# Hybrid sparse and dilated attention layer: QK-norm one item later in the projection, attention tiles from last to first

## The reference, cut to what matters

```
xn = rms_norm(x, norm_gain)
proj = xn @ w_in                       # 1024 -> 4420 columns
qa, ka, va, za, qi, ki, wi, qb, kb, vb, zb = split(proj)
qa, ka, qb, kb = per-head rms_norm (64 columns a head) times a gain
# A: indexer scores every causal key, keeps the 256 best of each query
score = sum_h relu(qi_h . ki) * wi_h ;  keep = top_k(score, 256)
a_out = softmax(qa . ka / 8 + bias, over keep) @ va
# B: dilated windows (128,1), (512,4), (2048,16), merged by their denominators
b_out = dilated_attention(qb, kb, vb)
out = x + concat(a_out * silu(za), b_out * silu(zb)) @ w_out
```

## Time and profile before

| | |
|---|---|
| median of 7 runs | 8387.62 us (8355.07 to 8503.0) |
| the profiled execution | 8384.74 us, its slowest core's span 8383.2 us |
| spans of the 8 cores | 8317.9 to 8383.2 us, granted clock 0.683 to 0.692 |
| busy in the span | TensorE 58%, VectorE 59%, ScalarE 67%, POOL 7% |
| projection | to about 1838 us |
| attention A of the first batch | 1846 to 4497 us, of the second 5104 to 7767 us |
| attention B and output projection | 4501 to 5098 us, and from 7770 us to the end |

### The profile page before, as it was taken

The page is one execution under the profiler, slowest core; times in us unless marked ns, Lnnn a source line. Parts: engine busy times, 40 slices in busy tenths (PEclk is TensorE's granted clock), DMA queues, the critical chain, the costliest instruction groups (busy, mean ns, idle before and its releaser), DMA issues. The chain is left out here.

```text
span 8383.2 us, 132302 instructions; the slowest of 8 cores (8317.9 to 8383.2 us)
## 1 busy us (share of the span) xinstructions
PE 4861.0 (58%) x40338; PEld 3177.5 (38%) x40338; DVE 4987.0 (59%) x9513; ACT 5648.6 (67%) x8477; POOL 598.8 (7%) x974
## 2 busy tenths in 40 slices
PE   3777667762455555555555962345555555556586
PEld 1332223321333444444444721233444444446452
DVE  2221222217777778777882655777877787775445
ACT  3655556755777788887885812677887888789551
POOL 2111111210000000000001100000000000000210
PEclk9877889985555556666667776555555566667769
DMA  5111212220000000000002474000000000000448
GB/s 159 68 64 61 68 62 75 74 92 24 23 16 28 18 21 20 21 23 22 25 2 74 143 247 147 26 15 26 19 20 33 21 12 14 24 23 3 129 141 281
DMA packets 249943, 494.53 MB, mean 59 GB/s; under 512 B 82016, under 2 KB 145408, under 8 KB 241568
## 3 DMA queue, kind: packets, MB, share of 16 engines
q1 hardware_dynamic: 192928, 314.06, 12.7%
q0 software_dynamic: 56320, 172.01, 5.5%
HBM read 313.99 MB, written 171.95 MB: 58 GB/s over the span
## 5 line engine op out<-in xcount | busy, mean ns | idle before, releaser
L194 DVE TENSOR_SCALAR_CACHE_REDUCE nm_u<-sc_u,cand_u 128x128 bf16<-128x128 f32 (+15 forms) x960 | 2245.2, 2339 | 1.7 <-issue 1.7
L185 ACT ACTIVATE nm_u<-sc_u,cand_u 128x256 bf16<-128x256 f32 (+15 forms) x960 | 2029.1, 2114 | 200.1 <-DVE cand_u L202 179.6
L176 PE MATMUL pb<-VA_s_u,pbuf_u 128*128 128x65 bf16 x8448 | 799.3, 227 | 2183.7 <-ACT pbuf_u L185 2179.9
L176 PEld LDWEIGHTS pb<-VA_s_u,pbuf_u 128*128 128x128 bf16 x8448 | 560.9, 117 | 2476.3 <-issue 2472.0
L176 PE MATMUL pb<-ident_u,nm_u 128*128 128x128 bf16 x6528 | 1389.9, 286 | 10.4 <-DVE nm_u L194 10.4
L176 PE MATMUL pb<-Qi_u,KaT_s_u 128*128 128x128 bf16 x6528 | 1376.5, 284 | 0.6 <-issue 0.2
L202 DVE SCALAR_TENSOR_TENSOR sc_u<-rbuf_u,wi_all_u,sc_u 128x512 f32<-128x512 f32 (+3 forms) x1152 | 813.7, 706 | 726.2 <-ACT rbuf_u L185 509.9
L185 ACT ACTIVATE pbuf_u<-pb,b_u 128x512 bf16<-128x512 f32 (+2 forms) x1728 | 1085.3, 664 | 4.7 <-PE pb L176 4.4
L185 ACT ACTIVATE rbuf_u<-pb 128x512 f32<-128x512 f32 (+3 forms) x1152 | 591.6, 560 | 560.9 <-PE pb L176 310.2
L176 PEld LDWEIGHTS pb<-ident_u,nm_u 128*128 128x128 bf16 x6528 | 862.8, 132 | 49.2 <-issue 37.2
L176 PEld LDWEIGHTS pb<-Qi_u,KaT_s_u 128*128 128x128 bf16 x6528 | 853.1, 131 | 7.9 <-issue 1.6
(11 more groups left out here) (100 smaller groups left out, 6672.3 us busy)
## 6 DMA issues: line engine op xcount, KB each, us to landing
Bres<-res_u POOLq DMA_DIRECT2D x192, 260.0 KB, 2.4
rr_u<-Bres SPq DMA_DIRECT2D x192, 260.0 KB, 7.4
xs_u<-x SPq DMA_DIRECT2D x64, 512.0 KB, 4.0
xf_u<-x SPq DMA_DIRECT2D x64, 512.0 KB, 5.3
out<-ot_u POOLq DMA_DIRECT2D x64, 512.0 KB, 7.1
vt_u<-Vb SPq DMA_DIRECT2D x192, 130.0 KB, 2.3
wst_u<-w_in SPq DMA_DIRECT2D x8, 2048.0 KB, 10.8
Va<-vst_u POOLq DMA_DIRECT2D x64, 130.0 KB, 2.6
```

The lines of the kernel that those rows point to most:

```text
L176: return lambda e: e.matmul(o, lhsT=l, rhs=r, start=start, stop=stop)
L185: return lambda e: e.activation(out=o, in_=i, func=func, scale=scale, **kw)
L194: return lambda e: e.tensor_scalar(out=o, in0=i, scalar1=s1, scalar2=s2, op0=op0, **kw)
```

## The change

Three things. In the projection the norm of an f item is split: its matmuls and the Square stay, and the rest (the `bones` matmul, Ln, Exp, multiply, store, or the copy of the other f items) is emitted behind the matmuls and the Square of the next f item. For that pf rotates over three PSUM tiles (pb0, pb1, pb3) and pS is pb2 alone. The items of a group are put in another order: the 8 VA and VB items stand between the first f items, then the other 11 f items in a row, then the 8 ZA and ZB items in a row; what is pending is emitted behind each ZA or ZB item. And the pairs of attention A go from m = 15 down to 0: A(15) alone, then A(m-1) with B(m), then B(0) alone.

```
@@ -430,7 +430,7 @@
-                pf = pb[kf % 2]
+                pf = (pb[0], pb[1], pb[3])[kf % 3]
...
@@ -438,8 +438,10 @@
                 if gc is not None:
-                    sq_, sd2, rs2, pS = sqb[kf % 2], sdb[kf % 2], rsb[kf % 2], pb[2 + kf % 2]
+                    sq_, sd2, rs2, pS = sqb[kf % 2], sdb[kf % 2], rsb[kf % 2], pb[2]
                     P.op("act", _act(sq_[:], pf[:], ACTF.Square), reads=[pf], writes=[sq_])
+                yield
+                if gc is not None:
                     P.op("pe", _mm(pS[:], bones[:], sq_[:], True, True), reads=[bones, sq_], writes=[pS])
...
@@ -486,16 +488,16 @@
+            pend = [None]
             for q in range(len(groups)):
+                vit = [("t", tt * 4 + j) for tt in range(4) for j in (0, 2)]
+                git = [("t", tt * 4 + j) for tt in range(4) for j in (1, 3)]
                 items = []
-                fi, ti = 0, 0
-                while fi < len(FM) or ti < 16:
-                    if fi < len(FM):
-                        items.append(("f", fi))
-                        fi += 1
-                    if ti < 16:
-                        items.append(("t", ti))
-                        ti += 1
+                for fi in range(len(FM)):
+                    items.append(("f", fi))
+                    if fi < len(vit):
+                        items.append(vit[fi])
+                items += git
...
                     if kind == "f":
-                        fm_item(q, v)
+                        gnew = fm_item(q, v)
+                        next(gnew)
+                        if pend[0] is not None:
+                            for _ in pend[0]:
+                                pass
+                        pend[0] = gnew
                     else:
                         tm_item(q, v // 4, v % 4)
+                    if (n_ == len(items) - 1 or (kind == "t" and v % 2 == 1)) and pend[0] is not None:
+                        for _ in pend[0]:
+                            pass
+                        pend[0] = None
...
@@ -712,12 +723,14 @@
-                for _ in stageA(0):
+                order = list(range(NP_ - 1, -1, -1))
+                for _ in stageA(order[0]):
                     pass
-                for m in range(NP_):
-                    ga = stageA(m + 1) if m + 1 < NP_ else iter(())
+                for oi, m in enumerate(order):
+                    mn = order[oi + 1] if oi + 1 < NP_ else None
+                    ga = stageA(mn) if mn is not None else iter(())
                     gbb = stageB(m)
-                    ua = unitsA(m + 1) if m + 1 < NP_ else 0
+                    ua = unitsA(mn) if mn is not None else 0
```

## The result

| | before | after |
|---|---|---|
| median of the runs compared | 8392.1 us (31 runs) | 8174.93 us (12 runs, 8112.75 to 8225.47) |
| ratio, 95% interval | | 0.9738, 0.9711 to 0.9765 |
| span of the profiled execution | 8383.2 us | 8145.4 us |
| table loads | 259 | 84 |
| core 6: first `kiT_u` load (projection done) | 1808.9 us | 1591.9 us |

A forecast was written before the change was run, and what follows sets the result against it. No engine was full: TensorE and ScalarE waited for each other in the projection, ScalarE and VectorE were nearly level in attention A. 8384.7 - 248 (projection) + 34 (attention) = 8171, forecast 8175 us, 8-in-10 range 8040 to 8320.

The forecast's parts named there:

- Table loads, 83: Projection, ScalarE: grouping the Silu leaves 83 table loads for 259, 226 us less ScalarE work.
- A late group, 74.5 us: Projection group without bias tables: 66.5 us of TensorE work plus waits, 74.5 for 88.1 us, 218 us in all.
- f items without a t item: Late group's last eight f items: TensorE waits for the norm chain to free pf, 3.3 us a group.
- among the Silu: Late group's Silu stretch: ScalarE's loads, Silu, Ln and Exp hold the fourth item's PSUM tile, 2.9 us of TensorE wait.
- Bias tables, 30 us: Projection's early groups: more TensorE items beside the first table's Exp hide its DMA trip, 30 us gained in all.
- Projection together, -248 us: Whole projection: 218 us from the groups and 30 from the bias tables, with bounds of 170 and 290 us.
- The three rotating tiles, the shared pS and the extra lists cost nothing more.: Projection: the new PSUM tile use and item lists add no cost, 0 us, unless ScalarE falls behind.
- The ends of attention, +107 a batch: Attention A's unpaired stages: A(15) 230 and B(0) 20 us replace A(0) 55 and B(15) 88, +107 us a batch.
- The middle, -90 a batch: Attention A's fifteen pairs: shorter by 90 us a batch, between ScalarE's -57 and VectorE's -169.
- 4 to 8 us shorter: Sign in attention A: each pair 4 to 8 us shorter than the pair of the same two numbers before.
- The lower clock at 0.81: Rival, projection: denser matmuls lower the mean clock to 0.81, late groups gain 2 us, total 8360 us; chance 0.09.
- fall to 0.70: Rival, projection: waits bring the mean clock to 0.70, projection +75 us, total 8494 us; chance 0.05.

The follow-up runs named there:

- The late Exp: The kernel after, with the Exp that ends a bias table issued at least 8 items behind the rest of its table: 8066.69 us, ratio 0.9624.
- the flush ahead of the Silu: The kernel after, with the last pending norm finished ahead of a group's first Silu item instead of behind it: 8147.36 us, ratio 0.9722.
- the late Exp and old items: The kernel before plus split norm, three tiles and bias Exp 8 items late; attention A up and down 8044.72 us, ascending 8098.95 us.

## Why the prediction came out

8175 us was forecast and 8174.93 measured. That the two agree so closely is luck: single runs of after lie between 8113 and 8225 us, and two terms were off and made up for each other.

- **Table loads, 83.** There are 84. That they were worth little, since TensorE binds, was said and is now shown from both sides: 207 fewer gave no gain that can be measured, 245 left standing took none of it away. What was wrong is the reading of the earlier trace rows, where I had the Square standing behind a load as the reason for the wait. The Square alone takes nearly that long.
- **A late group, 74.5 us.** 74.9 on core 6, term by term from the waits in four groups: f items without a t item 3.0 us (forecast 3.3), among the Silu 2.75 (2.9), for `sdb` 0.8 where 1.8 were allowed for other work of ScalarE. Against that TensorE's work is 68.4 us for 66.5: the matmuls that take 3.49 us for 1.89 are most of it, a term that the sum did not have. Two items of that chain take 5.07 us (5.03), from the start of the first of these rows to that of the last, in the timeline of after, core 6:

```profile
1480.87 1.89 PE L176 MATMUL pb<-xnT_u,W_u 128*128 128x512 bf16 x8
...
1484.00 1.89 PE L176 MATMUL pb<-xnT_u,W_u 128*128 128x512 bf16 x8 [1.03 <-DVE fst_u L202]
...
1485.94 1.89 PE L176 MATMUL pb<-xnT_u,W_u 128*128 128x512 bf16 x8
```

  The 0.25 + 0.52 us that the prediction calls the Square in this chain are not its time: the earlier trace rows have 0.60 for the Square, and 0.47 from the start of `bones` to that of the Ln. Against core 6's own late groups it is 12.9 us each, 206 in all for my 218.
- **Bias tables, 30 us.** This is the term that failed. Three tables cost 116.4 - 87.7 = 28.7 us a group before and 102.5 - 74.9 = 27.6 after: some 10 us in all. I had argued that four items of TensorE's work beside the Exp hide more of it than two. For two of the tables they do: in the early group shown above, ScalarE stands 8.9 and 10.5 us at their Exp, and TensorE waits at most 1.3 us at a time for `sdb` or `fst`. But the third Exp falls among the Silu, which I had seen and not priced high enough. The timeline of that group, after, core 6:

```profile
902.94 1.28 ACT L185 ACT_TABLE_LOAD   x1 [7.22 <-DMA NBf_u<-Rscr]
904.23 0.42 ACT L185 ACTIVATE EB_u<-NBf_u 128x256 bf16<-128x256 f32 x1
...
906.70 4.85 PE L176 MATMUL pb<-W_u,xnT_u 128*128 128x512 bf16 x11 [6.79 <-ACT gst_u L185]
```

  TensorE stands for 6.8 us behind it, and its waits for `gst` are 9.6 us in this group for 2.75 in a late one. That takes back what the two others give. The late Exp shows that this wait was the price.
- **Projection together, -248 us.** -217 on core 6, whose clock was not held (last section), -197 on core 3, which the forecast was made for.
- **"The three rotating tiles, the shared pS and the extra lists cost nothing more."** True and not enough. I had given the tiles no price for their absence; the third decides between -2.7% and +3.3%.
- **The ends of attention, +107 a batch.** +104 (226.3 and 20.9 for 230 and 20).
- **The middle, -90 a batch.** -123, a term mis-sized. It lay between ScalarE's -57 and VectorE's -169, and I had put it nearer to ScalarE; it came out a little nearer to VectorE. Net it is -18 and -27 a batch where I had +17, so on core 3 reversing the order gains 45 us (35 as a mean over all cores) rather than losing 34. This makes up for the projection. Of the three pairs shown, which were to be 4 to 8 us shorter, one is (4.7), and two are not (9.4 and 2.8).
- **The rivals.** The lower clock at 0.81 came true on two cores only: by the late groups it costs core 3 about 17 us, and its projection gains 20 us less than core 6's. What I had against this rival was misread. The row of 0.74 is not the least busy of the three (74.9 of 100 us; 84.0 of 118.9 at 0.87), and it comes from core 3 while that core was held at 0.81: by the clock records of its trace the group from 499 to 625 us ran 98 us at 0.81, 27 at 0.50 and none at full clock. The clock did not fall to 0.70. What that rival rested on is real all the same: with two tiles and no hold, core 3 ran a late group with 27 us of waits at 0.89, and the kernel was slower than before.

## What to carry to other kernels

Taking a dependent matmul back in an in-order queue paid here only with one tile more for what the later chain frees: count how many items lie between the last reader and the next writer, and price the split with and without it. Work removed from an engine that nobody waits for is worth little, however large its row: 207 table loads here, for a gain lost in the noise. And read the wait that ScalarE itself stands in (here a DMA trip behind an Exp): moving that one instruction by eight items gave more than the whole reordering of attention.

## What the hardware showed that I had not expected

**Two neighbouring cores, not all, are held at 0.81.** The window 1410 to 1460 us of after on cores 0 and 3 (columns as above, granted clock third from the end):

```profile
1410.00:1460.00 50.00, 46.82 (x253) 22.10 (x257) 13.65 (x23) 32.20 (x53) 12.95 (x24) 0.97 0.29 95
1410.00:1460.00 50.00, 48.24 (x201) 20.26 (x200) 16.02 (x23) 27.45 (x47) 11.10 (x20) 0.81 0.22 73
```

Core 2 shows 0.81 as well, the five others 0.97. Cores 2 and 3 end the projection at 1643 and 1650 us, the other six between 1578 and 1597. With the flush ahead of the Silu it is cores 4 and 5 (1674 and 1662 for 1552 to 1610), with the late Exp and old items again 4 and 5 (1580 and 1567 for 1479 to 1522), and a window of that kernel on core 4, 1300 to 1400 us, shows 0.81.

It does not need the denser projection. A window of before, 210 to 245 us, on cores 0 and 3, then 1400 to 1700 us on cores 0 and 2 of the kernel with the reversal alone, whose projection is the old one:

```profile
210.00:245.00 35.00, 24.54 (x119) 10.63 (x121) 10.33 (x16) 25.20 (x39) 7.02 (x13) 1.00 0.14 50
210.00:245.00 35.00, 29.05 (x119) 11.49 (x119) 8.68 (x13) 23.46 (x37) 6.04 (x12) 0.81 0.13 47
...
1400.00:1700.00 300.00, 253.22 (x1087) 104.84 (x1107) 68.79 (x107) 200.59 (x283) 58.12 (x107) 0.81 0.21 68
1400.00:1700.00 300.00, 235.12 (x1206) 103.94 (x1207) 75.75 (x121) 215.06 (x305) 66.16 (x120) 0.98 0.23 77
```

In before, cores 2 and 3 end the projection at 1840 and 1847 us and the others between 1800 and 1813; in the kernel with the reversal alone six cores end at 1890 to 1925 and cores 6 and 7 at 1817 and 1818. In the one with the projection's part alone no core's clock record has 0.81, and all end between 1573 and 1600. So by these ends the slowest core, which sets the time, loses from nothing to some 110 us to it, with the old projection and the new, and the medians of this document carry that. It is also why the late Exp shows more in the groups (the projection of cores 6 and 7 ends some 100 us earlier) than in the median (8145.61 to 8098.95). What picks the cores is not shown.
**A wait can cost twice.** In each of four late groups of after TensorE waits 2.35 us for the same `gst`. The 3 us behind it, core 6:

```profile
1273.60:1276.60 3.00, 2.97 (x16) 1.35 (x18) 0.00 (x0) 1.29 (x2) 1.19 (x3) 0.63 0.37 131
1349.30:1352.30 3.00, 3.00 (x8) 1.11 (x9) 0.00 (x0) 1.25 (x2) 1.15 (x3) 0.53 0.38 131
1424.70:1427.70 3.00, 2.97 (x8) 1.05 (x9) 0.00 (x0) 1.29 (x2) 1.48 (x3) 0.50 0.38 134
1500.20:1503.20 3.00, 2.92 (x21) 1.46 (x23) 0.16 (x1) 1.55 (x3) 1.13 (x3) 1.00 0.37 131
```

Three times the clock goes to its lower level, 1.2 GHz, for most or all of the stretch, and once it stays at 2.4; in the four late groups of the kernel with the new item order alone, waits of up to 2.2 us leave it at 1.00. So the price comes often behind a wait of this length, but not each time. With two tiles, where the waits are up to 4.4 us, it is 12 us a group on top of 27 us of waits (core 3).
